# Norms split off and spread out in a two-layer streaming encoder, with one reordered vector instruction in its attention

## The reference

```
h = rmsnorm(x, norm1_g); z = h @ w_in          # split among four head groups
o = [ MLA(z_a) | Diff(z_b) | SGU(z_c) | GDN(z_d) ]
x = x + o @ w_out
x = x + convffn(rmsnorm(x, norm2_g))
y = rmsnorm(x, final_g)                        # once, behind both layers
```

## Time and profile before

| | |
|---|---|
| median of 3 runs | 4158.48 us (4155.71 to 4162.19) |
| the profiled execution: its time, its span | 4157.04 us, 4155.3 us |
| PE busy | 3724.4 us, 90% of the span |
| DVE, ACT, POOL busy | 50%, 24%, 20% |
| mean granted clock of PE | 0.925 |

### The profile page before, as it was taken

One profiled execution on the slowest core, in us unless ns is written; L12 is line 12 of the kernel. 1 busy time (PEld: TensorE's weight loads), 2 busy tenths in 40 slices (PEclk: granted clock), 3 DMA queues, 4 the chain that ended last, 5 costly groups with the idle time before them and its releaser, 6 DMA issues. The chain is left out here.

```text
span 4155.3 us, 51971 instructions
## 1 busy us (share of the span) xinstructions
PE 3724.4 (90%) x21206; PEld 3361.4 (81%) x21206; DVE 2077.9 (50%) x3607; ACT 993.1 (24%) x1757; POOL 832.8 (20%) x716
## 2 busy tenths in 40 slices
PE   3978888889799999999878889887998999999996
PEld 2866876479699999999866668654987999999995
DVE  3355433255445565565544544424544555565554
ACT  2133223233221111111132322323323211111111
POOL 1211120011142222222122101100113332222230
PEclk8999999589799999999989999975998999999998
DMA  4512231010111111111053211201001111111111
GB/s 160 160 59 74 71 106 41 1 63 1 28 40 46 41 41 41 41 41 46 24 178 110 64 54 64 97 35 62 1 2 46 41 44 40 44 42 41 41 45 46
DMA packets 114240, 230.83 MB, mean 56 GB/s; under 512 B 33636, under 2 KB 76388, under 8 KB 110920
## 3 DMA queue, kind: packets, MB, share of 16 engines
q1 hardware_dynamic: 113992, 227.41, 17.5%
HBM read 172.81 MB, written 52.07 MB: 54 GB/s over the span
## 5 line engine op out<-in xcount | busy, mean ns | idle before, releaser
L256 PE MATMUL PS<-h_split,w_split 128*128 128x384 f32 x3072 | 1069.3, 348 | 63.0 <-PEq L195 61.3
L258 PE MATMUL PS<-h_split,w_split 128*128 128x384 f32 x3072 | 1046.5, 341 | 0.0
L257 PE MATMUL PS<-h_split,w_split 128*128 128x384 f32 x3072 | 1042.4, 339 | 0.0
L251 POOL TENSOR_TENSOR w_split<-w_full,w_split 128x1024 fp32r<-128x1024 f32 (+1 forms) x196 | 473.0, 2414 | 1101.2 <-ACT w_split L243 1101.2
L256 PEld LDWEIGHTS PS<-h_split,w_split 128*128 128x128 f32 x3072 | 588.8, 192 | 80.1 <-issue 74.4
L257 PEld LDWEIGHTS PS<-h_split,w_split 128*128 128x128 f32 x3072 | 585.0, 190 | 2.0 <-issue 0.3
L258 PEld LDWEIGHTS PS<-h_split,w_split 128*128 128x128 f32 x3072 | 584.4, 190 | 0.0
L243 ACT CAST w_split<-w_full 128x1024 fp32r<-128x1024 f32 (+1 forms) x196 | 203.8, 1051 | 1318.6 <-PE PS L258 1181.5
L2190 DVE TENSOR_TENSOR x<-x,PS 128x384 f32<-128x384 f32 x528 | 286.3, 552 | 180.8 <-PE PS L258 179.1
L256 PE MATMUL PS<-ffn_act,w_split 128*128 128x384 f32 x1056 | 365.7, 346 | 8.1 <-POOL w_split L251 7.1
L257 PE MATMUL PS<-ffn_act,w_split 128*128 128x384 f32 x1056 | 357.1, 338 | 0.0
(11 more groups left out here) (361 smaller groups left out, 5518.7 us busy)
## 6 DMA issues: line engine op xcount, KB each, us to landing
w_full<-in_w_up SPq DMA_DIRECT2D x88, 512.0 KB, 3.5
w_full<-in_w_down SPq DMA_DIRECT2D x44, 512.0 KB, 3.6
w_full<-in_w_in SPq DMA_DIRECT2D x40, 512.0 KB, 3.7
kq_keep<-split_rows SPq DMA_DIRECT2D x128, 128.0 KB, 2.4
kq_row<-kq_keep SPq DMA_DIRECT2D x32, 512.0 KB, 4.2
x_keep<-x SPq DMA_DIRECT2D x2, 4608.0 KB, 19.0
x<-x_keep SPq DMA_DIRECT2D x2, 4608.0 KB, 13.7
w_full<-in_w_out SPq DMA_DIRECT2D x16, 512.0 KB, 3.6
```

Source lines behind the costliest of these rows:

```text
L251: pool.tensor_tensor(ws[:, n % SSLOTS, 1, 0:w], wf[:, n % WSLOTS, 0:w], ws[:, n % SSLOTS, 0, 0:w].bitcast(F32), ALU.subtract).then_inc(w_l ...
L256: pe.matmul(out, w_hi, a_hi, start=first, stop=False)
L257: pe.matmul(out, w_hi, a_lo, start=False, stop=False)
L258: return pe.matmul(out, w_lo, a_hi, start=False, stop=last)
```

## The change

It has four parts; names on the left are of the new code.

1. **First norm.** `split_norm_stage` is gone. `start_stage` (the old setup stage, written anew) squares the blocks of `x` as they land, adds over the eight feature tiles by one `tensor_reduce` for each block, and inverts two of the three blocks. In the last down step of each layer the units run block by block instead of tile by tile; ACT squares each tile of `x` as it is finished, POOL adds the squares into `square_sums`, and PE, DVE and ACT turn two blocks into inverse roots under the products. The third block is finished in the next stage. `diff_stage` now holds what was left of the norm: DVE makes `h_rows` from `x`, `next_gain` and `square_sums`, and PE takes the first tile's products as the halves of each feature tile become ready, in the order `order`.
2. **Tiles preloaded.** The first two weight tiles of a layer are in `w_full` when it begins. `start_stage` copies them for both layers from DRAM to DRAM (`w_next`), four copies of 512 KB, since the address of a tile of the next layer is not an expression of the loop's register; the feed-forward stage loads from there. The store of `x` to `x_keep` is cut in three.
3. **Head norms.** Stage A is gone; its two tiles go with stage C. Silu of the first four tiles of `gdn_y` moves into `samples_stage`. The squares are now the weights of the matmul and the narrow matrix is what moves, so that sums stand in columns (a frame for each partition), DVE and ACT work on up to 24 columns, and PE transposes back, ACT copies, and PE spreads.
4. **Reordered combination.** In the attention, DVE combines unit `v` before it takes the maxima of unit `v + 1`.

`y_stage` takes its inverse roots from the last down step too, and stores `y` in six pieces. The core of the diff:

```diff
+            order = [(0, 0), (1, 0), (0, 1), (1, 1), (0, 2), (1, 2)]
+            order += [(n, b) for n in range(2, DIFF_TILES) for b in range(NB)]
...
+                    sp.dma_start(x_keep[:, 2:4, :], x[:, 2:4, :]).then_inc(xa, 16)
+                    sp.dma_start(par[:, :], d["par"][l]).then_inc(cin, 16)
+                    sp.dma_start(cst[:, :], d["consts"]).then_inc(cin, 16)
+                    sp.dma_start(x_keep[:, 0:2, :], x[:, 0:2, :]).then_inc(xb, 16)
+                    sp.wait_ge(flo, 1)
+                    w_load(sp, l, DQK_W + 2)
+                    sp.dma_start(x_keep[:, 4:8, :], x[:, 4:8, :]).then_inc(xc, 16)
+                    w_load(sp, l, DQK_W + 3)
+                    sp.wait_ge(xc, 16)
+                    sp.wait_ge(hf, KD * NB)
...
+                            if n == 0:
+                                pe.wait_ge((hld, hlp)[k % 2], b * KD // 2 + k // 2 + 1)
...
+                    pool.wait_ge(w_hid, 1)
+                    pool.tensor_tensor(ws[:, 0, 1, HALF_W:2 * HALF_W], wf[:, 0, HALF_W:2 * HALF_W],
+                                       ws[:, 0, 0, HALF_W:2 * HALF_W].bitcast(F32), ALU.subtract).then_inc(w_lod, 1)
+                    lows(0)
+                    w_low(pool, DQK_W + 1)
+                    lows(1)
+                    lows(2)
...
+                    def rows(b):
+                        for k in range(KD):
+                            j = b * KD + k
+                            if j >= 2 * KD and k % 2 == 1:
+                                dve.wait_ge(hlp, (j - 2 * KD) // 2 + 1)
+                            dve.scalar_tensor_tensor(out=full[:, j % (2 * KD), :], in0=x[:, k, b * BLK:(b + 1) * BLK],
+                                                     scalar=gnext[:, k:k + 1], in1=ss[:, b, :], op0=ALU.mult,
+                                                     op1=ALU.mult).then_inc(hf, 1)
+                            if b == 0 and k == 1:
+                                dve.wait_ge(fhi, 1)
+                                dve.tensor_tensor(ws[:, 0, 1, 0:HALF_W], wf[:, 0, 0:HALF_W],
+                                                  ws[:, 0, 0, 0:HALF_W].bitcast(F32), ALU.subtract).then_inc(flo, 1)
+                            if k >= 2 and k % 2 == 0:
+                                low(dve, b, k - 2).then_inc(hld, 1)
+                        low(dve, b, KD - 2).then_inc(hld, 1)
...
+                    rows(0)
+                    dve.wait_ge(smr, 1)
+                    invert_sums(dve, link, PS[:, 7, 0:BLK]).then_inc(rcd, 1)
+                    rows(1)
+                    dve.wait_ge(rtd, 1)
+                    rows(2)
...
+                        pe.wait_ge(sq_ready, (b + 1) * tiles)
+                        for t in range(PER):
+                            for n in range(tiles):
+                                u = b * tiles + n
+                                at_t = t * 8
+                                mm = pe.matmul(PS[:, b, at_t:at_t + rows], sq[:, u % SLOTS, t * P:(t + 1) * P],
+                                               C("head_put")[:, 8 * n:8 * n + rows], start=(n == 0), stop=(n == tiles - 1))
+                        mm.then_inc(sum_ready, 1)
...
+                        for t in range(PER):
+                            mm = pe.transpose(PS[0:rows, 3, t * P:(t + 1) * P], col[:, PER * b + t, 0:rows],
+                                              C("ident"))
+                        mm.then_inc(turned, 1)
...
-                            if v + 1 < U:
-                                maxima(v + 1)
-                            yield True
                             dve.scalar_tensor_tensor(out=Pb[:, v % 2, 0, 0:n], in0=Pb[:, v % 2, 1, 0:n],
                                                      scalar=stat[:, 2, v, 1:2], in1=Pb[:, v % 2, 0, 0:n],
                                                      op0=ALU.mult, op1=ALU.add).then_inc(w_ready, 1)
+                            if v + 1 < U:
+                                maxima(v + 1)
+                            yield True
...
+                    if c == LAST:
+                        return i % KD, i // KD
+                    return i // NB, i % NB
...
+                    for i in range(WSLOTS):
+                        sp.wait_ge(w_lod, W_TILES - WSLOTS + i + 1)
+                        sp.dma_start(wf[:, i, 0:KD * P], w_next[l, i]).then_inc(nwi, 16)
...
+                                if c == LAST and b >= 1 and m == 3:
+                                    pe.wait_ge(nsm, (KD - 1) * b)
+                                    pe.matmul(PS[:, b - 1, 0:BLK], ones[:, :], ss[:, b - 1, :], start=True,
+                                              stop=True).then_inc(nrd, 1)
...
+                    for i in range((KD - 1) * NB):
+                        b = i // (KD - 1)
+                        pool.wait_ge(nsq, i + 1)
+                        pool.wait_ge(nsm, i)
+                        pool.tensor_tensor(ss[:, b, :], ss[:, b, :], sq[i % 2][:, :], ALU.add).then_inc(nsm, 1)
...
+                                if c == LAST and b >= 1 and m == 5:
+                                    dve.wait_ge(nrd, b)
+                                    invert_sums(dve, link, PS[:, b - 1, 0:BLK]).then_inc(nrc, 1)
...
+                            if b == DEC_BATCH - 1:
+                                act.wait_ge(y_moved, 16)
+                                act.activation(y[:, 0, :], y[:, 0, :], ACT.Silu)
...
+                        for k in range(KD):
+                            dve.scalar_tensor_tensor(out=yT[:, k, cols], in0=x[:, k, cols], scalar=gnext[:, k:k + 1],
+                                                     in1=ss[:, b, :], op0=ALU.mult, op1=ALU.mult).then_inc(rows, 1)
+                        if b == 0:
+                            dve.wait_ge(smr, 1)
+                            invert_sums(dve, link, PS[:, 7, 0:BLK]).then_inc(rcd, 1)
...
+                        for t in range(WSLOTS):
+                            sp.dma_start(w_next[i, t], w_source((i + 1) % DEPTH, DQK_W + t)[0]).then_inc(kept_next, 16)
...
-            head_norm_stage(o_diff, 2, HD, 1e-5, lambda n: G("sub_g"), base=24, sums_of=s_col,
+            head_norm_stage([(y[:, n, :], HD ** -0.5 if n < 2 else 1.0, None) for n in range(4)], 1.0, EPS,
+                            late=(y[:, 4, :], y[:, 5, :]))
+            gdn_mix_stage(l)
+
+            def gather_sgu(sp):
+                sp.dma_start(o_sgu[:, :, :], sgu_keep).then_inc(kept_out, 16)
+                sp.wait_ge(kept_out, 48)
+
+            head_norm_stage([(o_diff[:, n, :], G("sub_g"), None) for n in range(2)]
+                            + [(y[:, n, :], G("gdn_g"), gate_b[:, n, :]) for n in range(2)], HD, EPS, sums_of=s_col,
                             prepare=lambda dve, link: link(dve.tensor_tensor(G("sub_g"), G("sub_g"),
-                                                                             G("one_minus_lam"), ALU.mult)))
-            head_norm_stage(y, 4, 1.0, 1e-6, lambda n: HD ** -0.5 if n < 2 else 1.0, base=24, silu=True)
-            gdn_mix_stage(l)
-            head_norm_stage(y[:, 0:2, :], 2, HD, EPS, lambda n: G("gdn_g"), base=24, gate=gate_b)
+                                                                             G("one_minus_lam"), ALU.mult)),
+                            load=gather_sgu)```

How the order moves on DVE in the attention (part 4), at a unit with 768 keys. `diff_stat` is the small tile of maxima and sums, `diff_P` the exponentials. Before:

```order
L1344 RECIPROCAL diff_stat<-diff_stat 128x1
L1345 TENSOR_SCALAR diff_stat<-diff_stat,lam 128x1
L1334 TENSOR_TENSOR PS<-PS,bias_p_451 128x256
L1335 TENSOR_REDUCE diff_stat<-PS 128x1
L1334 TENSOR_TENSOR PS<-PS,bias_p_451 128x256
L1335 TENSOR_REDUCE diff_stat<-PS 128x1
L1350 SCALAR_TENSOR_TENSOR diff_P<-diff_P,diff_stat 128x768
```

More of the change, by code:

```diff
@@ L705, in stack_copies, with invert_sums, diff_stage @@
             pool.tensor_copy(q_stack[:, m % 2], kq_row[:, 1]).then_inc(stacked, 1)
-        def diff_stage(l, bias_p, bias_s):
-            own = lambda n: "A"
+        def invert_sums(dve, link, s):
+            link(dve.tensor_scalar(s, s, 1.0 / D_MODEL, EPS, ALU.mult, ALU.add))
+            return dve.reciprocal(s, s)
+        def diff_stage(l, bias_p):
             halves = at("split_rows", [P, 2, 2, TOK], R(24), F32R)
+            full = at("h_rows", [P, 2 * KD, BLK], R(28))
+            order = [(0, 0), (1, 0), (0, 1), (1, 1), (0, 2), (1, 2)]
+            order += [(n, b) for n in range(2, DIFF_TILES) for b in range(NB)]
+            place = {nb: i for i, nb in enumerate(order)}
@@ L1003, in walk, with _ @@
                         back(b)
+                if load is not None:
+                    @block.sync
+                    def _(sp):
+                        load(sp)
                 @block.scalar
@@ L1067, in invert @@
                     def invert(b):
[L1068 to L1075 removed]
+                        dve.wait_ge(sum_ready, b + 1)
@@ L1076, in invert @@
```

(20 more changed lines are left out.)

497 lines of the change are left out of this document (242 added, 255 removed).

## The result

The changed kernel takes 4036.86 us (median of 4, 4033.59 to 4043.01) against 4157.39: ratio 0.971 (95% interval 0.9693 to 0.9727), 2.9% faster. The forecast was 4024 with 3972 to 4060 around it. The profiled execution has a span of 4036.9 us against 4155.3, 118.4 less where I had summed 134.7.

What follows compares the result with a forecast made beforehand. PE, busy 90% of the span, was taken as the bound, with the gain in short stages and waits where it idles. Terms 67.7 - 7 + 27 + 10 + 37 + 0 = 134.7 us gave 4024 us, range 3972 to 4060.

Steps and rivals of the forecast that it cites:

- First norm: First norm with the products behind it: 76.0 us becomes 42.6 in layer 0, gain 67.7 over both layers.
- the block of 10.8 us: First norm, per block: 6.4 us of DVE work and 4.4 of POOL subtractions, added rather than run side by side.
- the cover: Products for 25 us before the dv product, hiding its later weights; costed at nothing, a few us per layer if gone.
- The exclusion: First norm: DVE instructions with two SBUF inputs and POOL's SBUF reads wait for each other; without it, gain 17 larger.
- Last down step: End of each layer's feed-forward: added squares, two matmuls with ones and an inversion cost 3.5 us per layer, 7 in all.
- Final norm: Last stage: 48.3 us becomes 21 with 24 products, one inversion and the last store; gain 27.
- Head norms: Two stages per layer of 36 and 37.5 us at half clock, from 77.2 per layer; gain taken as 10, ends 7 and 51.
- Rival 2: Head norms hold the full clock, 41 us more gained: 3983 us; chance 16%.
- Combination: Attention: combining before the next unit's maxima removes PE's wait for it; gain 37 us, upper end 47.
- Rival 3: Attention hands its wait on, scores waiting for exponentials that wait for later maxima; half the gain lost, 4043 us; chance 13%.
- Setup: Setup stage, which ended at 44.5 us: change 0, from +6 to -10, with the DRAM-to-DRAM copies lying beside other work.
- rivals 4 and 5: Setup's DRAM-to-DRAM copies on one DMA engine: 87 us, 4102 (4%); or reading and writing in turn, 175 us, 4190 (3%).

Runs made afterwards that it cites:

- e3: Changed kernel with the first norm's inverse roots held in PSUM, ACT copying two blocks of them at the start; 4025.1 us (0.9689).
- e9: Changed kernel with all 24 subtractions of the first norm on DVE, none on POOL; 4044.6 us (0.9724).
- e11: Changed kernel with only the second inversion of the last down step moved behind its last addition, executed once; feed-forward stages 861.7 and 857.9 us.
- e2: Changed kernel with the head norms' sums as rows again, narrow matrix as weights and 384 columns moving; 4003.1 us (0.9638).
- e12: Changed kernel with the head norms' sums still in columns, but 128 columns instead of 8 moved behind each load; 4008.1 us (0.9654).
- e1: Changed kernel with the attention's combination back behind the next unit's maxima; 4080.3 us (0.9825).
- e6: Kernel before with only the combination put ahead of the next unit's maxima; 4112.8 us (0.9891).

## Why the prediction was right, point by point

**First norm: right in the sum by luck, wrong in two parts.** The copy of the sixth unit began at 80.65, 37.3 us after the stage's start, where I had 42.6. The step that failed is the block of 10.8 us: I added POOL's whole 1.10 us for each subtraction, but only 0.8 of it falls on DVE, and a block took 8.7 to 9.2. What this gave was lost at the end of the stage. "I cost that at nothing; if the cover is gone, a few us per layer" was said of `diff_stage`'s DMAs, and the cover was gone: from the sixth copy to the end were 56.0 us before and 61.5 now. So 5.3 us won and 5.5 lost cancelled in the 33.2 of layer 0, against 33.4 forecast. The exclusion itself stands (e3, e9); the forecast without it was 17 us better, and what removing its cause brought in the stages of e3 was 15.6.

**Last down step: mis-sized.** -3.5 per layer, measured -6.2 and -6.3, from stages that move by 2 to 3 us between traces. The inversion was "hidden by four PSUM banks except for about 0.5". That is right for the first inversion, which has five additions behind it to catch up, and wrong for the second, which has two. Its 2 us are in the trace of the kernel after; e11 shows that moving it gives back only 0.6 of them.

**Final norm.** 27 forecast, 28.0 without the gain's load.

**Head norms: the step that failed.** The two stages were to take 36 and 37.5 us at half clock and took 38.8 and 39.5. The spreading alone explains it, 3 us per stage: 5.49 each time where I had taken 4.5 as a mean of 2.84 and 5.48; the sums were exact (0.217 against 0.218 from the earlier trace rows). I had also taken the 77.2 us of layer 0 for both layers, and layer 1 had 75.3 before. From 73.5 I went to 72 because "the stages of before show 0.57 to 0.65, partly up"; but that was the row form. If the sums hold the clock down, the spreading behind them is slow as well, and the lower end of my range for this part, 7, should have been the middle at best; the measured -4.2 lies below it. Rival 2, the full clock, did not come. That the form is what costs, and not the clock of the neighbourhood, e2 and e12 show: the four stages took 156.7 us, and 116.6 in e2; the 40 us between them are about what the combination brought.

**Combination: right, and somewhat better.** 37 forecast, 42.4 measured, 42 to 45 in e1 and e6. The term was to be PE's wait alone. Of the 42.4 us, 29.1 are idle time of PE; the other 13.3 are its busy time in the same matmuls, at a granted clock of 0.96 and 0.97, where it was 0.95 in both layers before. I had not forecast that part. Rival 3, in which the wait is handed on to the scores, is refuted: that wait is 49.4 us, where it had 47.1. Its time, 4043, lies nearer to the measured one than mine, by 6 us against 13; only the trace separates them.

**Setup.** The stage ends at 43.3. The four copies from DRAM to DRAM did not lengthen it. DMA issues of the kernel after (count, size, median us to landing):

```profile
next_w<-in_w_in SPq DMA_DIRECT2D x4, 512.0 KB, 5.2
```

That is 5.2 us for 512 KB, where rivals 4 and 5 have 22 and 44 for each of four.

## What to carry to other kernels

Before a small reduction on TensorE is turned so that the data are the weights, look at what clock the stage has, and count the neighbours' slow-down too: here that form cost 20 us per layer in an edit that otherwise gained 18, and sixteen times the moved columns made it faster. When an engine's help runs beside DVE, put one of DVE's inputs in PSUM, or let the helper rest; adding an engine can take time away. And when a stage's start gets faster, read its end again: what was hidden behind the slow start (here 64 small stores in one queue) is what ends it next, and moving a single load in that queue brought 7 us over both layers, nearly half of what the faster norm of e3 brought.

## What was unexpected of the hardware

- 128 moved columns instead of 8 behind each 128x128 load made a stage 8.0 us of 38.8 shorter: 48 rows in 7.36 us instead of 10.41, at a granted clock of 0.67 instead of 0.50 over the stage.
- At a granted clock of 0.50 a row took 0.21 us with 128 columns (5.00 / 24) and 0.217 with 8 (10.41 / 48), and 24 rows together 5.49 and 5.29: behind a load of 128x128 weights in fp32 the added columns cost next to nothing. At 1.00 a row took 0.10 (3.00 / 30).
- Issuing a store of 128 KB took SP 0.7 to 0.8 us when alone, and 0.8 to 1.2 when ACT issued the same kind at the same time.
- A cast of 384 columns on DVE (0.35 us) took 2.56 beside a POOL subtraction, though it reads a single input.
